# Steps of two mixing stages moved between the moments of a weight stream, a bias moved from TensorE to VectorE, and one norm split by token tile

## The reference: what is computed

```python
o_b = (rms_norm(o_b, b_sub_norm[l].reshape(B_HEADS, B_V_DIM)) * (1.0 - lam_init))
```

## Time and profile before

| | us |
|---|---|
| median of three executions | 2862.9 |
| the three executions | 2861.51, 2862.90, 2863.93 |
| the profiled execution, its own time | 2862.68 |
| its span (first to last instruction) | 2860.5 |

### The profile page before, as it was taken

One profiled execution on the slowest core, in us unless ns is written; L12 is line 12 of the kernel. 1 busy time (PEld: TensorE's weight loads), 2 busy tenths in 40 slices (PEclk: granted clock), 3 DMA queues, 4 the chain that ended last, 5 costly groups with the idle time before them and its releaser, 6 DMA issues. The chain is left out here.

```text
span 2860.5 us, 56704 instructions
## 1 busy us (share of the span) xinstructions
PE 2675.8 (94%) x17336; PEld 2400.1 (84%) x17336; DVE 2047.0 (72%) x4600; ACT 1493.3 (52%) x2943; POOL 176.1 (6%) x136
## 2 busy tenths in 40 slices
PE   7989999989997899799999999988999899999997
PEld 6859988779976899799988888777998899888886
DVE  5757767657767668877767777777579777677776
ACT  5545556544554455456655555544454566555554
POOL 0000000000000034300000000000244000000000
PEclk9999999999998999999999999989999999999999
DMA  5225654236552467555567777624576555577775
GB/s 195 82 60 169 184 154 163 71 98 188 180 173 89 155 192 229 168 173 174 174 202 231 235 232 235 209 79 147 171 229 200 157 174 174 183 231 235 232 233 181
DMA packets 194304, 503.48 MB, mean 176 GB/s; under 512 B 22560, under 2 KB 88352, under 8 KB 192800
## 3 DMA queue, kind: packets, MB, share of 16 engines
q1 hardware_dynamic: 194208, 502.28, 55.9%
HBM read 467.59 MB, written 34.60 MB: 176 GB/s over the span
## 5 line engine op out<-in xcount | busy, mean ns | idle before, releaser
L182 DVE TENSOR_TENSOR w_lo<-w_raw,w_hi 128x512 fp32r<-128x512 f32 (+1 forms) x1464 | 994.9, 683 | 369.5 <-ACT w_hi L173 349.7
L173 ACT ACTIVATE w_hi<-w_raw 128x512 fp32r<-128x512 f32 (+2 forms) x1592 | 926.6, 621 | 208.4 <-PE banks_right L217 136.7
L215 PE MATMUL up_up<-hT_hi,w_hi 128*128 128x256 f32 x2048 | 595.9, 291 | 26.6 <-DVE w_lo L182 20.5
L217 PE MATMUL up_up<-hT_hi,w_lo 128*128 128x256 f32 x2048 | 582.9, 285 | 0.0
L216 PE MATMUL up_up<-hT_lo,w_hi 128*128 128x256 f32 x2048 | 582.6, 284 | 0.0
L215 PEld LDWEIGHTS up_up<-hT_hi,w_hi 128*128 128x128 f32 x2048 | 396.2, 193 | 31.0 <-DVE w_lo L182 23.8
L227 PE MATMUL banks_left<-w_hi,expert_hi 128*128 128x512 f32 x1024 | 407.6, 398 | 7.8 <-DVE w_lo L182 7.8
L228 PE MATMUL banks_left<-w_lo,expert_hi 128*128 128x512 f32 x1024 | 406.9, 397 | 0.0
L229 PE MATMUL banks_left<-w_hi,expert_lo 128*128 128x512 f32 x1024 | 406.9, 397 | 0.0
L216 PEld LDWEIGHTS up_up<-hT_lo,w_hi 128*128 128x128 f32 x2048 | 395.8, 193 | 0.0
L217 PEld LDWEIGHTS up_up<-hT_hi,w_lo 128*128 128x128 f32 x2048 | 395.2, 193 | 0.0
(11 more groups left out here) (376 smaller groups left out, 3960.1 us busy)
## 6 DMA issues: line engine op xcount, KB each, us to landing
w_raw<-in_peer_u_c SPq DMA_DIRECT2D x256, 512.0 KB, 3.5
w_raw<-in_peer_v SPq DMA_DIRECT2D x256, 512.0 KB, 3.6
w_raw<-in_w_up_c SPq DMA_DIRECT2D x88, 512.0 KB, 3.7
expert_gelu_held<-expert_gelu SPq DMA_DIRECT2D x256, 128.0 KB, 1.7
expert_back<-expert_gelu_held SPq DMA_DIRECT2D x256, 128.0 KB, 3.3
w_raw<-in_w_down SPq DMA_DIRECT2D x44, 512.0 KB, 4.1
w_raw<-in_w_in_r SPq DMA_DIRECT2D x40, 512.0 KB, 3.7
w_raw<-in_w_in_c SPq DMA_DIRECT2D x32, 512.0 KB, 3.5
```

What stands on the lines that cost most here:

```text
L173: self.nc.scalar.activation(self.w_hi[:, k % SLOTS, 0:width], self.raw_half(k, width), ACT.Copy).then_inc(self.sem("w_hi_done"), 1)
L182: self.nc.vector.tensor_tensor(self.w_lo[:, k % SLOTS, 0:width], self.raw_half(k, width), self.w_hi[:, k % SLOTS, 0:width].bitcast(F32), A ...
L215: self.nc.tensor.matmul(bank, hi, self.hT_hi[:, c, :], start=(c == 0), stop=False)
L217: last = self.nc.tensor.matmul(bank, lo, self.hT_hi[:, c, :], start=False, stop=(c == DC - 1))
```

## The change

In `FirstMiddle`:

- The alibi bias is no longer a product on TensorE. `biggest` on VectorE adds it in place to the scores in PSUM before it finds the maximum.
- `PAUSES` has one empty moment ahead of each of the halves 54, 56, 58 and 60 in place of three ahead of 62. `LAST_SPLITS` and `splits` split halves 62 and 63 at the empty moment 67 and run four ahead from half 60 on.
- The norm of the differential attention is done for each token tile: the first tile's root stands at moment 65 on ScalarE and its scaling at 66 on VectorE. Mix job 17 is due at moment 69 and job 18 at moment 70, behind half 62.

In `SecondMiddle`:

- Nearly all steps of the attentions stand one to three moments earlier (the first scores at 20 instead of 22), the turned heads of the window attention go to banks of the output accumulator, and the order of some steps differs.
- The taps are taken earlier: the last at moment 36 instead of 42. Both convolutions are transposed at moments 37 and 38, into different banks. The pause ahead of half 48 is gone.
- The squares of the mixes are taken by ScalarE instead of VectorE. ScalarE's sigmoid of the gate stands behind the copies of the latents.
- Halves 36 and 37 wait for what they need of their banks instead of everything.

The diff, cut to its core; first `FirstMiddle` with its helpers, and the constants and waits of `SecondMiddle`:

```diff
AHEAD = 2
-    PAUSES = {52: 4, 62: 3}
+    PAUSES = {52: 4, 54: 1, 56: 1, 58: 1, 60: 1}
+    LAST_SPLITS = (67, 60)
     WA = (A_HEADS + A_KV) * A_DIM
...
         return 2 * j + 1 if what == "col" else 2 * len(self.tiles) + DC * (j + 1) - 1
+    def splits(self, v, k):
+        early, first = self.LAST_SPLITS
+        if k is None:
+            return (first + 2, first + 3) if v == early else ()
+        ahead = self.AHEAD if k < first else self.AHEAD + 2
+        return (k + ahead,) if EARLY <= k + ahead < self.nh else ()
...
         for v, k in enumerate(self.moments()):
-            if k is not None and EARLY <= k + self.AHEAD < self.nh:
-                K.split_hi(act, self.k0h + k + self.AHEAD, self.widths[k + self.AHEAD])
+            for j in self.splits(v, k):
+                K.split_hi(act, self.k0h + j, self.widths[j])
             for j in range(nt):
...
-        def scores(job, q, k, bias):
+        def scores(job, q, k):
...
             for u in range(2):
-                ins = T.matmul(dst[:, u, :], q(u), k(u), start=True, stop=(bias is None))
-                if bias is not None:
-                    ins = T.matmul(dst[:, u, :], ident, bias, start=False, stop=True)
+                ins = T.matmul(dst[:, u, :], q(u), k(u), start=True, stop=True)
             ins.then_inc(S["s_in"], 1)
...
                 b_values(s - 4)
+        yield 69
         mix_job(17, (3, 4), (S["mixed"], 3))
+        yield 70
         mix_job(18, (5,), (S["mixed"], 3))
...
+        def root_b(t):
+            act.wait_ge(S["ms"], 4 + t)
+            A.activation(self.rt[:, 3, t, 0:B_HEADS], self.ms[:, 3, t, 0:B_HEADS], ACT.Sqrt).then_inc(S["root"], 1)
         def mix_hi(job, chunks):
...
                 turned(6 + s - 2, 9 + s - 2, 1)
-        root(3, B_HEADS, 4)
+            if s == 8:
+                root_b(0)
+        yield 67
+        root_b(1)
+        yield 69
         act.wait_ge(self.out_gains, 1)
         mix_hi(17, (3, 4))
+        yield 70
         mix_hi(18, (5,))
...
-        def biggest(g, job, scale):
+        def biggest(g, job, scale, bias=None):
             dve.wait_ge(S["s_in"], job + 1)
+            if bias is not None:
+                link(V.tensor_tensor(self.s_bank(job), self.s_bank(job), bcast_mid(bias, 2), ALU.add))
             link(V.tensor_reduce(self.top[:, g, :], self.s_bank(job), AX.X, ALU.max))
...
             link(add_up(3, mix_b, t, B_HEADS))
+            ms = self.ms[:, 3, t, 0:B_HEADS]
+            V.tensor_scalar(ms, ms, 1.0 / B_V, EPS1, ALU.mult, ALU.add).then_inc(S["ms"], 1)
+        def b_normed(t):
+            dve.wait_ge(S["root"], 4 + t)
+            link(V.reciprocal(self.ms[:, 3, t, 0:B_HEADS], self.rt[:, 3, t, 0:B_HEADS]))
+            scaled(self.ob, mix_b, 3, t, B_HEADS).then_inc(S["mixed"], 1)
...
             if s < 8:
-                biggest(6 + s, self.ATT_B + s, B_DIM ** -0.5)
+                biggest(6 + s, self.ATT_B + s, B_DIM ** -0.5, self.alibi[:, s // 4, s % 4, :])
             if 1 <= s <= 8:
...
                 b_out(0)
+            if s == 10:
+                b_normed(0)
         b_out(1)
-        mean(3, B_HEADS, B_V)
-        inverse(3, B_HEADS, 4)
-        for t in range(TT):
-            scaled(self.ob, mix_b, 3, t, B_HEADS).then_inc(S["mixed"], 1)
+        b_normed(1)
+        yield 69
         dve.wait_ge(self.out_gains, 1)
         mix_lo(17, (3, 4), 5)
+        yield 70
         mix_lo(18, (5,), 7)
...
     AHEAD = 2
-    PAUSES = {48: 3}
+    PAUSES = {}
     CF_TILES, SC_TILES = (8, 9, 6, 7), (2, 3, 4, 5, 0, 1)
...
     MW, SW = ROW2[0][1], ROW2[1][1]
-    TAPS = {17: 2, 18: 2, 19: 2, 20: 2, 21: 2}
+    TAPS = {16: 1, 17: 2, 18: 2, 19: 2, 23: 2, 24: 2, 25: 2, 29: 1, 30: 2, 31: 2, 32: 2, 36: 2}
...
                 c = self.OUT_ORDER[i]
-                if i == 0 and h == 0:
-                    pe.wait_ge(self.row_free, 4)
-                    pe.wait_ge(self.col_free, 10)
+                if i == 0:
+                    pe.wait_ge(S["heads_out"], 7)
+                    pe.wait_ge(self.col_free, 9 + h)
                 if h == 0:
```

The steps of `SecondMiddle` on TensorE, ScalarE and VectorE, in this order:

```diff
-        yield 22
+        yield 20
         pe.wait_ge(S["heads_out"], 4)
         scores(0, 0)
-        yield 23
+        yield 21
         scores(1, 1)
-        yield 24
+        yield 22
         pe.wait_ge(S["biased"], 1)
...
         turn(0)
-        yield 25
-        pe.wait_ge(S["biased"], 2)
+        yield 23
+        turn(1)
+        yield 24
         pe.wait_ge(self.row_free, 4)
-        s_pair(0, 1)
-        turn(1)
-        yield 26
-        pe.wait_ge(S["biased"], 3)
-        s_pair(1, 0)
+        s_pair(0)
+        s_pair(1)
         turn(2)
         values(0)
+        yield 25
+        pe.wait_ge(S["heads_out"], 5)
+        s_pair(2)
+        values(1)
+        yield 26
+        pe.wait_ge(S["biased"], 2)
+        pe.wait_ge(S["heads_out"], 7)
+        scores(3, 1)
+        values(2)
         yield 27
-        pe.wait_ge(S["heads_out"], 5)
-        s_pair(2, 1)
-        values(1)
+        pe.wait_ge(S["biased"], 3)
+        scores(4, 0)
         yield 28
-        pe.wait_ge(S["heads_out"], 7)
-        scores(3, 0)
-        values(2)
+        pe.wait_ge(S["biased"], 4)
+        scores(5, 1)
+        turn(3)
         yield 29
-        scores(4, 1)
+        turn(4)
         yield 30
-        pe.wait_ge(S["biased"], 4)
-        scores(5, 0)
-        turn(3)
-        yield 31
-        turn(4)
-        yield 32
         turn(5)
         values(3)
-        yield 33
+        yield 31
         values(4)
-        yield 34
+        yield 32
         values(5)
...
         pe.wait_ge(S["freed"], 2)
-        turn_convs(0)
+        turn_convs(0, self.o_bank)
+        mix_job(1)
         yield 38
-        mix_job(1)
-        yield 42
+        pe.wait_ge(S["biased"], 5)
+        pe.wait_ge(S["tapped"], CF_K + 1)
+        turn_convs(2, self.s_bank(0))
+        yield 41
         mix_job(2)
-        yield 43
-        pe.wait_ge(S["tapped"], CF_K + 1)
-        turn_convs(2)
-        yield 49
+        yield 46
         mix_job(3)
...
         yield 12
-        act.wait_ge(self.col_free, 2)
-        A.activation(self.gate[:], self.chans[:, 8:10, :], ACT.Sigmoid).then_inc(S["sig"], 1)
-        yield 13
         act.wait_ge(S["lat_turned"], 1)
...
         A.activation(self.latT[:, 2, :], self.s_bank(1)[:, 0:SEQ], ACT.Copy).then_inc(S["lat_out"], 1)
-        yield 16
+        act.wait_ge(self.col_free, 2)
+        A.activation(self.gate[:], self.chans[:, 8:10, :], ACT.Sigmoid).then_inc(S["sig"], 1)
+        yield 15
         act.wait_ge(S["q_up"], 2)
...
-        yield 18
+        yield 17
         act.wait_ge(S["kv_up"], 2)
...
+        def squares(i, src):
+            A.activation(self.sq[:], src, ACT.Square).then_inc(S["sq"], 1)
         def root(i):
...
-        yield 20
+        yield 18
         for j in range(2):
             heads(j, self.mT[:, 2 * j:2 * j + 2, :], self.s_bank(j))
-        yield 21
+        yield 19
         for j in range(2):
             heads(2 + j, self.mT[:, M_HEADS + 2 * j:M_HEADS + 2 * j + 2, :], (self.t_bank, self.o_bank)[j])
+        yield 21
+        exps(0)
+        yield 22
+        exps(1)
         yield 23
-        exps(0)
-        yield 24
-        exps(1)
-        yield 25
         exps(2)
         turned(0)
-        yield 26
-        heads(4, self.sT[:, 0:2, :], self.s_bank(1))
+        yield 24
         turned(1)
+        for j in range(2):
+            heads(4 + j, self.sT[:, 2 * j:2 * j + 2, :], self.acc[:, j])
+        yield 25
+        turned(2)
+        heads(6, self.sT[:, 4:6, :], self.acc[:, 0])
         yield 27
-        heads(5, self.sT[:, 2:4, :], self.s_bank(0))
-        turned(2)
+        exps(3)
         yield 28
-        heads(6, self.sT[:, 4:6, :], self.s_bank(1))
+        exps(4)
+        act.wait_ge(S["freed"], 1)
+        squares(0, self.mix[:, :, 256:512])
         yield 29
-        exps(3)
-        yield 30
-        exps(4)
-        yield 31
         exps(5)
         turned(3)
-        yield 32
+        yield 30
         turned(4)
         root(0)
+        yield 31
+        turned(5)
         yield 33
-        turned(5)
-        yield 35
         mix_hi(0)
+        yield 34
+        act.wait_ge(S["freed"], 2)
+        squares(1, self.mix[:, :, 768:1024])
         yield 36
...
         yield 38
+        mix_hi(1)
         act.wait_ge(S["conv_turned"], 1)
-        A.activation(self.sq[:].rearrange("p t n -> p (t n)"), self.o_bank, ACT.Square).then_inc(S["sc_sq"], 1)
-        yield 39
-        mix_hi(1)
+        squares(2, self.o_bank.rearrange("p (t n) -> p t n", t=TT))
         yield 40
         root(2)
-        yield 43
-        mix_hi(2)
-        yield 45
         act.wait_ge(S["cf_var"], 1)
         A.activation(self.std[:], self.moms[:, :, 1], ACT.Sqrt, bias=eps).then_inc(S["cf_std"], 1)
-        yield 46
+        yield 42
+        mix_hi(2)
         act.wait_ge(S["cf"], 1)
         A.activation(self.mix[:, :, 512:768], self.cf[:], ACT.Silu).then_inc(S["silu"], 1)
```

(66 more changed lines are left out.)

40 lines of the change are left out of this document (18 added, 22 removed).

## The result

The kernel before has a median of 2862.2 us in the comparison with the changed one (2860.65 to 2863.93). The changed kernel ran four times there (median 2831.5, 2826.15 to 2835.31; ratio to before 0.9891, 95% interval 0.9870 to 0.9913) and four times more as a control (median 2829.5, before 2862.0 beside it). The eight executions together have a median of 2829.5: **some 32 us less, 1.1%**. The forecast was 2822, the range 2802 to 2848.

A forecast was written before the change was run, and what follows sets the result against it. TensorE, busy 94% of the span, was taken as the bound, and in the second block a loop through three engines. 2862.7 - 16.0 (first block) - 24.8 (second block) = 2821.9, forecast 2822 us, range 2802 to 2848.

The forecast's parts named there:

- (a): First block, each layer: the alibi bias products leave TensorE, 8 steps and 32 records, 11.2 us busy.
- (b): First block: VectorE gets 8 in-place PSUM additions of 128x512, 0.69 us each, 0.72 us to a dependent operation.
- rival of the slow add: Rival: each new first-block addition takes 1.18 us instead of 0.72, +7.4 us, 2829 us; chance 0.04.
- (c): First block's attention with fewer output halves beside it: last value product ends after 32.9 us instead of 41.6.
- the walk: Moment-by-moment count of engine steps and waits; at full clock, first-block stage 48.1 us and second block's end at 921.0.
- (d): First block after the last value product: 15.2 us at full clock plus 2.9 for clock falls, 18.1 against 17.4.
- (e): Second block up to moment 16: half 16 at 836.8 instead of 836.4, so nothing gained.
- (f): Second block, moment 16 to the last tap: VectorE nearly always busy, last tap at 897.5 instead of 918.3.
- (h): Second block's clock: two falls cost 3.1 and 1.5 us; end 925.6 against 938.0, -12.4 us a layer.
- (g): Second block, last tap to the end: half 48 at 915.0, end at 921.0, before clock falls.
- clock rival: Rival: the clock stays up in the new, shorter waits, -10.9 and -17.0 us a layer, 2807 us; chance 0.17.
- The stalls only move: Rival: second-block waits only move to other moments and only the first block gains, 2847 us; chance 0.13.

The follow-up runs named there:

- experiment 6: Changed kernel plus seven zero-operand products on TensorE in the waits of the first block's attention; 2818.05 us, ratio 0.9849.
- experiment 4: Kernel before with one edit: the first block's alibi bias added by VectorE, halves and norm as they were; 2846.1 us, ratio 0.9948.
- 10 to 12: Changed kernel with experiment 8's exchange and filler products in both blocks, 2809.0 us; with experiment 4's first block and fillers instead, 2806.1; that plus norm by tile, 2806.3.
- experiment 7: Experiment 6 plus five and four filler products ahead of two second-block waits for turned probabilities; 2812.2 us, ratio 0.9830.
- experiment 8: Changed kernel with ScalarE's second-block copies of turned probabilities, groups 0 and 3, put ahead of the exponentials of groups 2 and 5; 2821.6 us, ratio 0.9861.

## Why the prediction was right, and where it was not

The direction, the range and most terms held; the gain was forecast at 41 us and is 32 (36 in the profiled execution).

- **(a), (b) bias.** The 11.2 us a layer went. The addition takes 0.70 us and 0.73 to the next, forecast 0.69 and 0.72. So the rival of the slow add is out.
- **(c) attention.** Forecast: last value product after 32.9 us. With the waits filled and at full clock it is 32.8 (experiment 6). The waits at the pauses are 1.3, 1.1 and 2.4 us against 0.3, 1.2 and 2.3, that for the output bank 0.5 against 1.5. But the changed kernel took 36.4 and 40.6. **This is the step that failed**: the sum charges the clock 2.9 us a layer, in the tail, set off by the 3.8 us that I expected idle at the last pause, and nothing inside the attention. It cost 3.6 and 7.8 us there. Waits of 1 to 2.4 us were enough, in every one of the eight stages of the changed first block that were traced without fillers (clock 0.79 to 0.90 over the stage). In five of them the clock fell already at or just behind the first pause, whose wait the walk had at 0.3 us; in layer 1 of the changed kernel:

```profile
546.35:549.75 3.40, 2.82 (x8) 2.14 (x8) 3.23 (x9) 2.56 (x11) 0.00 (x0) 0.51 0.17 67
```

- **(d) tail.** 14.8 us against 15.2, and the 2.9 us set aside for the clock were not needed, since it was 1.00 there in this profile. So the two mistakes cancel in layer 0 (51.2 against 51.0), which is luck, and not in layer 1 (55.4).
- **The placing of halves.** The sum charged its pauses (5.3 us of waits) and credited its tail, but never set the result beside the bias edit alone. Experiments 4 and 10 to 12 show that this edit carries the whole gain, but for the 0.5 us of the norm by tile.
- **(e)** Half 16 starts 26.0 and 25.4 us after half 0, forecast 25.4: nothing, as said.
- **(f), (h) last tap.** The walk has it 60.7 us after half 16 (its sum adds the 57.1 us of work to 836.4 and not to its own 836.8, a slip of 0.4), and (h) adds up to 4.6 for the clock. Measured are 66.6 and 65.2 with the clock as it was, and 63.8 in both layers at full clock (experiment 7). So the walk was 3 us short. VectorE's work was right (57.9 us against 57.1), and so was the sum of its waits with the clock (8.7 and 7.3 us against 4.0 + 4.6), but not their places. I had 2.7 us for the first window scores, which took 1.3. Most of the waits (5.9 us in layer 0) are for ScalarE's high parts, for which the walk had only the 1.3 us that it set down for everything else. The claim that TensorE's waits "are mostly hidden, because VectorE is the later one" fell with experiments 7 and 8. TensorE's waits themselves were well placed: 3.7 and 3.2 us, forecast 3.2 and 3.6; 1.6 at the convolution's transposes, forecast 2.0.
- **(g) to the end.** From the last tap it is 23.6 and 22.8 us, and 23.5 were forecast. The end stands 90.2 and 88.0 us after half 16, forecast 88.8. Here two misses cancel, and the good total is luck in part: at full clock it stands 86.6 us after half 16 (experiment 7), 2.4 more than the walk's 84.2, while the clock, charged with 4.6, cost 3.6 in layer 0 and 1.4 in layer 1.
- **Rivals.** The clock rival pointed the wrong way in the first block: it let the clock stay up, while there it fell further than in the forecast. "The stalls only move" is half true: of 9.0 us for the copies 6.8 are left.

Open: why the same program, with the same waits, gets a clock of 0.79 over a stage in one execution and 0.90 in another. The profiles show when it falls, not what decides it. Shorter fillers, or fillers away from the waits, were not tried. So it isn't shown how little filling is enough, nor which of the waits matters.

## What to carry to other kernels

Before giving work that TensorE does without waiting to another engine, ask what the granted clock will be in the gaps that this leaves: short waits (5.3 us in all in the first block's attention) cost another 3.6 and 7.8 us here in clock, and seven products a layer that compute nothing gave back some 10 us. When a change joins a simple edit with a new order, time the simple edit alone first: here it gave all of the gain in the first block. A wait on one engine is hidden only if no other engine waits behind it with work for the one that you take for the bound: here TensorE's wait reached VectorE through ScalarE's queue. And when a fix changes both an order and the clock, find a run that changes only one of them, as experiment 7 does for experiment 8.

## What the runs showed of the hardware that was not expected

- One program without a change scattered over 2826 to 2835 us with its mean granted clock (0.979 to 0.975). The six filled kernels stayed within 2.2 to 4.4 us each; but with four or five executions of each that shows little, for two kernels without fillers did too (3.0 us in experiment 4, 3.6 in experiment 8).
- One us at 1.2 GHz instead of 2.4 cost 0.4 us in these stages, where TensorE is busy for some 85% of the time: 51.2 us with 10.2 us of it, 56.9 with 23.9, from the same instructions.
- A granted clock of 0.75 over 40.6 us, half of that stretch at 1.2 GHz, with no single idle time of TensorE above 2.4 us in it.
- Products into an output bank with a zero operand between those that accumulate there cost 0.53 us each of TensorE's busy time (3.7 us for seven) and left the stage otherwise as it was.
- An addition of VectorE in place in PSUM, 128x512, costs what a read of the same width costs, 0.70 us against 0.69, and what depends on it starts 0.73 us behind its start.
